# Three spare strips of 128 bytes per partition between the operands of a two-block float32 kernel

## What is computed

```python
def _swiglu(h, w_in, w_out):
    gate, up = jnp.split(h @ w_in, 2, axis=-1)
    return (jax.nn.silu(gate) * up) @ w_out

def conv_ffn(h, w_up, conv_w, conv_b, w_down):
    s = h.shape[1]
    u = h @ w_up
    up = jnp.pad(u, ((0, 0), (CONV_WIDTH - 1, 0), (0, 0)))
    conv = conv_b
    for j in range(CONV_WIDTH):
        conv = conv + conv_w[j] * up[:, j:j + s]
    a, g = jnp.split(conv, 2, axis=-1)
    return (jax.nn.silu(a) * g) @ w_down

for li in range(DEPTH):                      # first block, DEPTH = 2
    g = norm_gains[li]
    x = x + 0.5 * _swiglu(_rmsnorm(x, g[0]), ffn_w_in[li, 0], ffn_w_out[li, 0])
    h = _rmsnorm(x, g[1])
    ...                                      # x = x + HGRN2 mixer (li 0) or MLA mixer (li 1) of h
    x = x + 0.5 * _swiglu(_rmsnorm(x, g[2]), ffn_w_in[li, 1], ffn_w_out[li, 1])
    gate = jax.nn.sigmoid((_rmsnorm(x, g[3]) @ ple_w_gate[li]).astype(jnp.float32))
    x = x + (gate * (p[li] @ ple_w_in[li]).astype(jnp.float32)).astype(x.dtype)
for layer in range(DEPTH):                   # second block
    ...                                      # x = x + stick-breaking attention and pooling, or gated linear attention
    x = x + conv_ffn(rms_norm(x, ffn_norm[layer]), ffn_w_up[layer], ffn_conv_w[layer],
                     ffn_conv_b[layer], ffn_w_down[layer])
```

## The kernel before

| buffers | byte in the partition, first of them | modulo 512 |
|---|---|---|
| `raw0` to `raw2` | 16512 | 128 |
| `x`, `x_hi`, `x_lo` | 41088 | 128 |
| `h_hi`, `h_lo`, `h_val`, `c_hi`, `c_lo` | 65664 | 128 |
| `q_both`, `x_lo_2` | 75904 | 128 |
| `par` | 92288 | 128 |
| `cst` | 94304 | 96 |
| `w_hi0` to `w_hi2`, `w_lo0` to `w_lo2`, `tmp` | 113344 | 192 |
| `work`, `small` | 172768 | 224 |

## Time and profile before

### The profile page before, as it was taken

How to read it: one execution, slowest core, us unless ns; L and a number is a source line. 1 busy time by engine, 2 the same in 40 slices (tenths; PEclk the granted TensorE clock), 3 DMA queues, 4 the chain that set the end, 5 groups by cost and what they waited for, 6 DMA issues and landing times.

```text
span 1825.6 us, 36701 instructions
## 1 busy us (share of the span) xinstructions
PE 1757.0 (96%) x14498; PEld 1721.6 (94%) x14498; DVE 1191.0 (65%) x1765; ACT 957.9 (52%) x1100; POOL 351.8 (19%) x280
## 2 busy tenths in 40 slices
PE   7999989989999899999999999989899999989998
PEld 7999989989999899998998999988899999989998
DVE  6655589976565665556456555665487776567776
ACT  5444667775444754444345444465455455655553
POOL 2000500030004600026663000566400011020001
PEclk9999999999999999999999999999999999999999
DMA  6656323335555365543434555434245454345552
GB/s 217 209 184 243 132 96 116 116 116 186 201 187 190 111 224 190 201 144 133 138 138 148 187 188 185 173 120 154 97 162 206 165 192 139 116 162 184 185 205 92
DMA packets 45168, 298.25 MB, mean 163 GB/s; under 512 B 5024, under 2 KB 5408, under 8 KB 15920
## 3 DMA queue, kind: packets, MB, share of 16 engines
q1 hardware_dynamic: 45104, 297.38, 46.0%
HBM read 296.31 MB, written 1.05 MB: 163 GB/s over the span
## 4 chain that ended last, share of the span: by engine, by line
PE 82%; DVE 10%; ACT 4%; issue 3%; DMA 1%; POOL 0%; SPq 0%; DVEq 0%; ACTq 0%
PE wk L379 15%; PE wk L380 15%; PE wk L381 15%; PE acc L379 8%; PE acc L380 8%; PE acc L381 8%; DVE x_lo L457 1%; PE wk L391 1%; PE wk L390 1%; PE wk L389 1%; PE wk L1043 1%; DVE sumsq L690 1%; DVE x L422 1%; ACT w_hi L325 1%; DVE w_lo L351 1%
## 5 line engine op out<-in xcount | busy, mean ns | idle before, releaser
L325 ACT ACTIVATE w_hi<-raw 128x2048 fp32r<-128x2048 f32 (+5 forms) x300 | 533.3, 1787 | 406.6 <-PE wk L381 337.7
L380 PE MATMUL wk<-x_lo,w_hi 128*128 128x256 f32 x2560 | 718.3, 281 | 0.0
L379 PE MATMUL wk<-x_hi,w_hi 128*128 128x256 f32 x2208 | 627.4, 284 | 21.4 <-DVE x_lo L457 16.5
L2618 POOL TENSOR_TENSOR w_lo<-raw,w_hi 128x512 fp32r<-128x512 f32 (+1 forms) x274 | 351.0, 1315 | 1459.0 <-ACT w_hi L325 1458.9
L381 PE MATMUL wk<-x_hi,w_lo 128*128 128x256 f32 x2208 | 620.6, 281 | 0.0
L351 DVE TENSOR_TENSOR w_lo<-raw,w_hi 128x2048 fp32r<-128x2048 f32 (+2 forms) x218 | 484.1, 2222 | 169.0 <-ACT w_hi L325 168.8
L380 PEld LDWEIGHTS wk<-x_lo,w_hi 128*128 128x128 f32 x2560 | 484.3, 189 | 0.3
L379 PEld LDWEIGHTS wk<-x_hi,w_hi 128*128 128x128 f32 x2208 | 422.9, 192 | 27.6 <-DVE x_lo L457 18.8
L381 PEld LDWEIGHTS wk<-x_hi,w_lo 128*128 128x128 f32 x2208 | 419.5, 190 | 0.0
L379 PE MATMUL acc<-h_hi,w_hi 128*128 128x256 f32 x1376 | 391.3, 284 | 16.3 <-DVE h_lo L2207 4.7
L380 PE MATMUL acc<-h_lo,w_hi 128*128 128x256 f32 x1376 | 387.7, 282 | 0.0
(11 more groups left out here) (325 smaller groups left out, 2140.5 us busy)
## 6 DMA issues: line engine op xcount, KB each, us to landing
raw<-w_ffn_loop SPq DMA_DIRECT2D x120, 1024.0 KB, 4.8
raw<-w_conv_loop SPq DMA_DIRECT2D x60, 1024.0 KB, 4.8
raw<-w_mla_loop SPq DMA_DIRECT2D x18, 768.0 KB, 4.2
raw<-w_hgrn_loop SPq DMA_DIRECT2D x10, 896.0 KB, 4.5
raw<-w_ple_gate SPq DMA_DIRECT2D x8, 1024.0 KB, 4.7
raw<-w_odd_loop SPq DMA_DIRECT2D x10, 768.0 KB, 4.3
raw<-w_even_loop SPq DMA_DIRECT2D x6, 1024.0 KB, 4.8
raw<-w_odd_proj SPq DMA_DIRECT2D x6, 1024.0 KB, 4.8
```

What stands on the lines that cost most here:

```text
L325: nc.scalar.activation(w_hi[slot][:, 0:n], raw[slot][:, 0:n], ACT.Copy).then_inc(S("hi_ready"), 1)
L379: nc.tensor.matmul(dst, hi, a_hi, start=start, stop=False, skip_group_check=True)
L380: nc.tensor.matmul(dst, hi, a_lo, start=False, stop=False, skip_group_check=True)
L2618: last = nc.gpsimd.tensor_tensor(w_lo[slot][:, a:b], raw[slot][:, a:b], w_hi[slot][:, a:b].bitcast(F32), ALU.subtract)
```

## The change

Three tensors that nothing reads or writes are declared between others. Each takes 32 float32 elements, 128 bytes, of every partition.

```diff
@@ -236,11 +236,13 @@
         x = sb("x", [P, KD, SEQ])
         x_hi = sb("x_hi", [P, KD, SEQ], F32R)
         x_lo = sb("x_lo", [P, KD, SEQ], F32R)
+        sb("gap_x_h", [P, 32])
         h_hi = sb("h_hi", [P, 2, SEQ], F32R)
         h_lo = sb("h_lo", [P, 2, SEQ], F32R)
         h_val = sb("h_val", [P, 2, SEQ])
         c_hi = sb("c_hi", [P, 2, SEQ], F32R)
         c_lo = sb("c_lo", [P, 2, SEQ], F32R)
+        sb("gap_h_x2", [P, 32])
         q_both = sb("q_both", [P, KD, SEQ], F32R)
         x_lo_2 = sb("x_lo_2", [P, KD, SEQ], F32R)
         par = sb("par", [P, N_PARAMS])
@@ -250,6 +252,7 @@
         sumsq = sb("sumsq", [P, SEQ])
         ln_ms = sb("ln_ms", [P, SEQ])
         ln_tok = sb("ln_tok", [P, 2 * TB])
+        sb("gap_x2_w", [P, 32])
         w_hi = [sb(f"w_hi{s}", [P, SLOT_TILES * P], F32R) for s in range(SLOTS)]
         w_lo = [sb(f"w_lo{s}", [P, SLOT_TILES * P], F32R) for s in range(SLOTS)]
         tmp = sb("tmp", [P, 8, SEQ])
```

## The result

The changed kernel takes 1843.26 us (median of 4 runs, 1841.0 to 1856.53) against 1820.34 us before (1817.8 to 1830.26): a ratio of 1.0125, with a 95% interval of 1.0081 to 1.0168. It is slower by 22.9 us, beyond the interval. The profiled execution has a span of 1839.1 us, against 1825.6 us before.

A forecast was written before the change was run, and what follows sets the result against it. The prediction took TensorE's matmul spacing as the bound. Address change and other engines at 0 left 1825.6 us for the profiled execution; the median, 1820.55 + 0 and a little over, became 1822 us, range 1804 to 1846.

The forecast's parts named there:

- rival B: TensorE's matmuls: places decide and the new ones are worse; all tiles slow gives 1846 us, 1.4% over the median; chance 0.12.
- within 1%: Whole kernel: time within 1% of before, chance 0.72; slower by over 1% had 0.13, faster 0.15.
- What bounds the kernel: TensorE, matmuls busy 96% of 1825.6 us: the bound is matmul spacing, with two paces 4.5 ns apart.
- Other engines at 0: Rounding (L325), VectorE's subtraction (L351) and GpSimd's (L2618): new weight places cost 0, slack covering a small difference.
- The draw of paces: Loops: each phase falls into its pace by history; one flipped loop is worth 6.4 us, the median 1811 to 1837.
- Which value I take: TensorE's matmuls: the pace follows interruptions, with addresses as bystanders, so the change of address costs 0.
- four pieces of evidence: ffn0 against ffn1, a flip in ple0, mla's loop, token against channel tiles: place modulo 512 does not choose the pace.
- A: TensorE's matmuls: places decide and the new ones are better; all tiles fast gives 1792, 1.6% under the median; chance 0.14.
- C: The h products: places act for one of three groups alone, 11 us less or 7 us more; chance 0.08.
- D: Buffer places: strips do not do what they say; x products mostly get a mirror image; no separate size or chance.

The follow-up runs named there:

- x192_h64: Strips of 128 bytes between x and h and of 128 bytes ahead of the weights, against the kernel before: 1827.54 us against 1815.55 us, ratio 1.0056.
- w_plus448: One strip of 448 bytes ahead of the weights, none elsewhere, against the kernel before: 1865.53 us against 1820.4 us, ratio 1.0238.
- lead_64: One strip of 64 bytes ahead of all buffers, against the kernel before: 1810.68 us against 1815.28 us, ratio 0.9979.
- w_plus384: One strip of 384 bytes ahead of the weights in place of the change's three, against the kernel before: 1849.21 us against 1828.56 us, ratio 1.0126.
- w_plus256: One strip of 256 bytes ahead of the weights, against the kernel before: 1819.8 us against 1815.28 us, ratio 1.0019.
- w_plus64: One strip of 64 bytes ahead of the weights, none elsewhere, against the kernel before: 1847.21 us against 1820.4 us, ratio 1.0155.

## Why the prediction was partly right

The number, 1822 us in a range from 1804 to 1846, holds the measured 1843.26 us, but only because the range was widened to take in rival B. The likeliest case, "within 1%" at 0.72, did not come true, and the one which did had 0.13.

**What bounds the kernel.** Right. TensorE's spacing of matmuls was the only thing that the change touched. The 4.5 ns between the two paces is what separates the loops, or the products in them, in every kernel at 64 or 192.

**Other engines at 0.** Right: L325, L351 and L2618 kept their durations within 1% (1787 to 1783, 2222 to 2222, 1315 to 1320 ns).

**The draw of paces.** Right in that loops flip, and larger than the three runs had shown: they spread over 12.5 us, and the same kernel ran from 1808 to 1833 us over the comparisons. That the draw is history alone was wrong, since the relation sets its odds.

**"Which value I take": 0 for the change of address.** This is the step that failed: it cost 13.5 us between the profiled executions and 22.9 us between the medians. The four pieces of evidence proved less than I read in them. Three showed both paces at one set of addresses. That shows that addresses do not decide alone, and I took it to mean that they do not matter. They leave open that the addresses set which paces are possible and how often each is fallen into, which is what the runs show. The kernel before sits at 192 modulo 256, the only relation of those tried at which most loops could be at 113 ns. I had compared relations within one kernel whose channel tiles all have the same one, so three of the four pieces could not have shown a dependence. The one piece that could, the token tiles with the mirrored relation at 118 ns, pointed to the loss. I noted it and set it aside, because 118 ns occurs at the old relation too. The same trace would have given it more weight: all seven groups of 48 such matmuls were at 117.8 ns, while the loops' channel tiles had both paces. It would not have settled it, as shorter groups of token tiles had both too.

**The rivals.** B was the right one in its direction, its place (x products at the mirrored relation) and its point of decision (ffn1 and, in part, ffn2 turned slow). Its price was 21.0 us over the profiled execution with every tile slow, 1846.6 us. The profiled execution of the change has 1839.1 us: the h products of ffn2 kept the fast pace, and five groups of token tiles gained it. B had the h products wrong, which it put in the middle of the matmul, 320 bytes apart; modulo 256 they did not move. B's mechanism, two reads which collide, was not tested. That all loads are long at 0 modulo 256 fits it, but the x products of the change are slow with no long load, so the loads' length does not bear it out. A did not occur at any of the relations tried. C's assumption, that the places act for each group of products by itself, is shown by the changed kernel's ffn2 and by x192_h64, though they act in all three groups, each by its own relation, and not in one alone. D was set aside with the remark that the x products get "a mirror image" and that this goes with the forecast. The mirror image is what costs: 64 and 192 are not alike.

The rule of the Trainium skill that I cited, that on the engines' side only the port pair which VectorE and GpSimd share causes contention (SBUF — State Buffer, section "SBUF: two separate sides"), would have given 0 for the change and for all twelve experiments. The same instructions take up to 45 us more by place alone (w_plus448, 1865.53 against 1820.4 us). The measurement decides.

**What stays open.** What makes the pace depend on the relation was only argued, never tested. The runs don't tell why one loop at 192 falls into one pace and another into the other, nor why 64 falls into the fast one so seldom. Whether a relation off the multiples of 16 bytes does better than 192 was not tried, nor 16 bytes off 64. No kernel that ran beats the kernel before: lead_64 has the same relation, and its interval includes 1.

## What to carry to other kernels

When TensorE loads weights for each matmul, as here with 128 and 256 columns of float32r, divide a stretch of time by its number of matmuls. If the result differs between stretches with the same work and clock, lay the moving and stationary buffers at several distances modulo 256 bytes and time each. The cost of a bad distance is a few ns per matmul, and here 1.2 to 2.4% of the kernel. Evidence that a quantity varies with the suspected cause held fixed does not clear the cause: it can still set the odds.

## What the runs showed of the hardware

- The spacing of float32r matmuls with 256 columns, each with its own weight load, depends on the start of the moving minus that of the stationary operand, modulo 256 bytes: at 0 it was 119.8 ns in all loops, at 96 119.8, at 128 118.5, at 160 117.1 or 118.5, at 224 118.2, with 176 and 208 in one kernel 118.3 on average, and at 64 and 192 113.1 or 117.6 ns (windows' counts, clock 1.00).
- 256 bytes more between the operands change nothing (1.0019, 0.9988 to 1.005), nor do 64 bytes ahead of everything (0.9979, 0.9948 to 1.001), but 16 or 32 bytes between them do.
- At 192 and 64 there are two paces for the same code and addresses, kept in some loops for about 1400 matmuls on end, and swapped at interruptions as short as that of 0.22 us in the earlier trace rows. Where the products of one loop have different relations, the pace can also change from one product to the next and back without an interruption (the changed kernel's ffn2, conv0 of x192_h64). The odds differ: token tiles at 192 were fast in 12 of 14 groups of 48 (the change, w_plus384), at 64 in none of 28 (the kernel before, w_plus256, lead_64, x192_h64), while groups of 12 had both paces at either relation.
- The length of a weight load does not give the pace: 188 ns at 113.1 ns, one of three at 192 ns at 117.6 ns with a relation of 192, but none longer than 188 ns on average at 117.6 ns with a relation of 64, and none at 118.5 ns in w_plus64. All are at 192 ns at 119.8 ns with a relation of 0.
